# Moving the output transposes of a sliding-window attention two steps on, and a group's compressed scores to another PSUM place, in a two-block fp32 kernel

## What is computed

```
s = einsum('tghd,cgd->tghc', qt, k_cmp) * scale        # the compressed scores, 31 keys
p_cmp = masked_softmax(s, ...)
o_cmp = einsum('tghc,cgd->tghd', p_cmp, v_cmp)
...                                                     # o_slc, o_win in the same way over 512 keys
o = gt[:, 0] * o_cmp + gt[:, 1] * o_slc + gt[:, 2] * o_win
```

```
parts = [sink_col, s_ctx, where(band_ok, s_lat, NEG_INF)]
p = softmax(concatenate(parts))
o = einsum(p_ctx, vc) + einsum(p_lat, vb)               # (128 tokens) x (16 heads x 64)
```

## Time and profile before

| | us |
|---|---|
| median of 3 runs | 3192.96 |
| lowest and highest | 3188.86 and 3198.78 |
| the profiled execution's own time | 3198.71 |
| its span, first to last instruction | 3196.6 |
| mean granted TensorE clock in it | 0.975 |

### The profile page before, as it was taken

One profiled execution on the slowest core, in us unless ns is written; L12 is line 12 of the kernel. 1 busy time (PEld: TensorE's weight loads), 2 busy tenths in 40 slices (PEclk: granted clock), 3 DMA queues, 4 the chain that ended last, 5 costly groups with the idle time before them and its releaser, 6 DMA issues.

```text
span 3196.6 us, 41132 instructions
## 1 busy us (share of the span) xinstructions
PE 3018.4 (94%) x16349; PEld 2571.3 (80%) x16349; DVE 1659.3 (52%) x2849; ACT 1178.3 (37%) x2056; POOL 286.5 (9%) x274
## 2 busy tenths in 40 slices
PE   7999999887889999999888999999999999999999
PEld 5788888765778888887677888888888889888887
DVE  7767666668676666641445744222222655343333
ACT  4632223435673322331444643211112545442222
POOL 2410001001562000010000110000000100010001
PEclk9999999998999999999998999999999999899999
DMA  4235444242003444421000101111111210022231
GB/s 141 95 111 171 149 161 145 86 147 79 1 1 106 145 162 155 158 80 43 9 19 26 32 33 58 64 62 64 62 66 61 62 32 1 27 86 98 88 104 67
DMA packets 76286, 260.19 MB, mean 81 GB/s; under 512 B 8256, under 2 KB 12864, under 8 KB 75968
## 3 DMA queue, kind: packets, MB, share of 16 engines
q1 hardware_dynamic: 76096, 257.57, 24.1%
HBM read 255.44 MB, written 2.10 MB: 81 GB/s over the span
## 4 chain that ended last, share of the span: by engine, by line
PE 49%; DVE 3%; ACT 3%; issue 2%; DVEq 0%; ACTq 0%
PE PS L517 47%; PE PS L1416 2%; DVE SM L2450 0%; PE PS L1450 0%; ACT TMP L1423 0%; DVE PS L2250 0%; DVE SM L2120 0%; ACT TMP L1407 0%; ACT WH L439 0%; DVE QRS L1905 0%; DVE NKL L2174 0%; ACT PB L1423 0%; ACT PB L1407 0%; ACT N L2159 0%; DVE WL L445 0%
## 5 line engine op out<-in xcount | busy, mean ns | idle before, releaser
L439 ACT ACTIVATE WH<-RAW 128x1024 fp32r<-128x1024 f32 (+1 forms) x367 | 379.5, 1037 | 843.9 <-PE PS L517 557.6
L517 PE MATMUL PS<-UH,WH 128*128 128x512 f32 (+1 forms) x1664 | 602.4, 362 | 33.0 <-DVE UL L971 12.7
L445 DVE TENSOR_TENSOR WL<-RAW,WH 128x1024 fp32r<-128x1024 f32 (+1 forms) x367 | 446.4, 1220 | 340.2 <-ACT WH L439 329.3
L517 PE MATMUL PS<-UL,WH 128*128 128x512 f32 (+1 forms) x1664 | 590.7, 355 | 0.0
L517 PE MATMUL PS<-UH,WL 128*128 128x512 f32 (+1 forms) x1664 | 588.0, 353 | 0.0
L517 PEld LDWEIGHTS PS<-UH,WH 128*128 128x128 f32 x1664 | 317.6, 191 | 89.0 <-issue 16.3
L517 PEld LDWEIGHTS PS<-UL,WH 128*128 128x128 f32 x1664 | 317.5, 191 | 47.6 <-issue 5.9
L517 PEld LDWEIGHTS PS<-UH,WL 128*128 128x128 f32 x1664 | 316.4, 190 | 45.2
L658 POOL TENSOR_TENSOR ACC<-ACC,TMP 128x256 f32<-128x256 f32 (+1 forms) x108 | 117.6, 1104 | 2091.5 <-ACT TMP L648 2090.1
L517 PE MATMUL PS<-XSH,WH 128*128 128x512 f32 (+1 forms) x752 | 284.2, 378 | 5.2 <-ACT TMP L815 2.5
L517 PE MATMUL PS<-XSL,WH 128*128 128x512 f32 (+1 forms) x752 | 283.1, 376 | 0.0
(11 more groups left out here) (350 smaller groups left out, 5383.7 us busy)
## 6 DMA issues: line engine op xcount, KB each, us to landing
RAW<-in_mod_w SPq DMA_DIRECT2D x96, 512.0 KB, 3.3
RAW<-in_f_in SPq DMA_DIRECT2D x88, 512.0 KB, 3.4
RAW<-in_g_in SPq DMA_DIRECT2D x88, 512.0 KB, 3.2
RAW<-in_f_out SPq DMA_DIRECT2D x32, 448.0 KB, 3.8
RAW<-in_g_out SPq DMA_DIRECT2D x32, 448.0 KB, 3.1
RAW<-in_a_in SPq DMA_DIRECT2D x16, 512.0 KB, 3.9
RAW<-in_f_out SPq DMA_DIRECT2D x16, 512.0 KB, 4.0
RAW<-in_g_out SPq DMA_DIRECT2D x16, 512.0 KB, 3.2
```

What stands on the lines that cost most here:

```text
L439: act.e.activation(hi, raw, ACT.Copy).then_inc(wh.step(n, i), 1)
L445: dve.e.tensor_tensor(lo, raw, hi.bitcast(F32), ALU.subtract).then_inc(wl.step(n, i), 1)
L517: return pe.e.matmul(out, l, r, start=start, stop=stop)
```

## The change

In the sliding-window attention, `flip_tensor`, `flip_high` and `flip_low` of a query block go from step n+4 to step n+6, n being its last unit; the loops of the engines run to step 69 (before, PE and ACT to step 68 and DVE to step 67). `OST2` becomes two buffers of 1024 columns, at another address; a block's first output waits for the transposes of the block two before.

In the sparse attention, the compressed scores are made in the "aux" place that query blocks 1 and 3 use, in two pieces: the mask and the products of query blocks 0 and 1 (five) at the end of step n-3, those of query blocks 2 and 3 (four) at the end of step n-2. The first group's stay in one piece. ACT's copy to `CS` stays where it was.

```diff
-    OST2 = at("OST2", U0 + 44 * KB, [128, 1024])
+    OST2 = at("OST2", U0, [128, 2, 1024])
...
-         "score": [("lin", 0), ("lin", 1)], "across": [("lin", 2)], "half": [("half", 0), ("half", 1)]},
+         "score": [("lin", 0), ("lin", 1)], "across": [("lin", 2)], "half": [("half", 0), ("half", 1)], "compressed": [("aux", 0)]},
...
-        nsa_compressed(pe, 0)
+        psum.rings["compressed"] = [psum.rings["aux"][(psum.turn["aux"] + 1) % 2]]
+        nsa_compressed(pe, 0, (0, 1, 2, 3))
...
+            if s + 3 in CMP[1:]:
+                nsa_compressed(pe, s + 3, (0, 1))
             if s + 2 in CMP[1:]:
-                nsa_compressed(pe, s + 2)
-
-    def nsa_compressed(pe, n):
+                nsa_compressed(pe, s + 2, (2, 3))
+
+    def nsa_compressed(pe, n, blocks):
...
         g = NW[n].g
-        o = psum.enter("half", "compressed", g)
-        pe.wait_ge(*psum.clear("compressed", g), act_q.after("kp", 1), dve_q.after("nsa", 2 * g + 1, 1, "lo"))
-        mm(pe, o[:, 0:512].rearrange("p (t n) -> p t n", t=4), IDR[:, :], CMR[:, :].unsqueeze(1).to_broadcast([128, 4, 128]), True, False)
-        for q in range(4):
+        if blocks[0] == 0:
+            o = psum.enter("compressed", "compressed", g)
+            pe.wait_ge(*psum.clear("compressed", g), act_q.after("kp", 1), dve_q.after("nsa", 2 * g + 1, 1, "lo"))
+            mm(pe, o[:, 0:512].rearrange("p (t n) -> p t n", t=4), IDR[:, :], CMR[:, :].unsqueeze(1).to_broadcast([128, 4, 128]), True, False)
+        o = psum.at["compressed", g]
+        for q in blocks:
             c, x = slice(96 + 128 * g - 32 * q, 224 + 128 * g - 32 * q), Q2[:, q, 4 * g:4 * g + 4, :]
             mm(pe, o[:, 0:512], KPH[:, c], x, False, False)
             last = mm(pe, o[:, 0:512], KPL[:, c], x, False, q == 3)
-        last.then_inc(score.step("compressed", g), 1)
+        last.then_inc(score.step("compressed", g, blocks[-1]), 1)
...
-        for s in range(len(SWA) + 5):
+        for s in range(len(SWA) + 6):
...
-            n = s - 4
+            n = s - 6
             if 0 <= n < len(SWA) and SWA[n][1] == 15:
-                flip_tensor(pe, ("swa", SWA[n][0]), OST2, 8, [fin.after("swa", n)])
+                flip_tensor(pe, ("swa", SWA[n][0]), OST2[:, SWA[n][0] % 2, :], 8, [fin.after("swa", n)])
...
-                dve.wait_ge(outp.after("swa", n), recip.after("swa", n), *([flip.after(("swa", q - 1), 4)] if q else []))
+                dve.wait_ge(outp.after("swa", n), recip.after("swa", n), *([flip.after(("swa", q - 2), 4)] if q > 1 else []))
...
-                if h == 15:
-                    flip_low(dve, ("swa", q), flipped_hi(q), flipped_lo(q), 8)
+            n = s - 6
+            if 0 <= n < len(SWA) and SWA[n][1] == 15:
+                q = SWA[n][0]
+                flip_low(dve, ("swa", q), flipped_hi(q), flipped_lo(q), 8)
```

More of the change, by code:

```diff
@@ L1664, in compressed_scalar @@
     def compressed_scalar(act, g):
-        act.wait_ge(score.after("compressed", g), *([score.after("nsa", CMP[g - 1])] if g else []))
+        act.wait_ge(score.after("compressed", g, 3), *([score.after("nsa", CMP[g - 1])] if g else []))
         act.e.activation(CS[:, :], psum.at["compressed", g][:, 0:512], ACT.Copy).then_inc(act_q.step("compressed", g), 1)
@@ L2444, in swa_vector @@
     def swa_vector(dve):
-        for s in range(len(SWA) + 4):
+        for s in range(len(SWA) + 6):
             n = s - 1
@@ L2459, in swa_vector @@
                 q, h = SWA[n]
-                dve.wait_ge(outp.after("swa", n), recip.after("swa", n), *([flip.after(("swa", q - 1), 4)] if q else []))
-                dve.e.tensor_scalar(OST2[:, 64 * h:64 * h + 64], psum.at["outp", "swa", n][:, 0:64], stat_of(n)[:, 4:5], None,
+                dve.wait_ge(outp.after("swa", n), recip.after("swa", n), *([flip.after(("swa", q - 2), 4)] if q > 1 else []))
+                dve.e.tensor_scalar(OST2[:, q % 2, 64 * h:64 * h + 64], psum.at["outp", "swa", n][:, 0:64], stat_of(n)[:, 4:5], None,
                                     ALU.mult).then_inc(fin.step("swa", n), 1)
                 psum.leave(("outp", "swa", n), fin)
-                if h == 15:
-                    flip_low(dve, ("swa", q), flipped_hi(q), flipped_lo(q), 8)
+            n = s - 6
+            if 0 <= n < len(SWA) and SWA[n][1] == 15:
+                q = SWA[n][0]
+                flip_low(dve, ("swa", q), flipped_hi(q), flipped_lo(q), 8)
     def tensor_engine(pe):
```

## The result

| | before | changed |
|---|---|---|
| median of 11 runs, us | 3195.26 | 3185.85 |
| lowest and highest | 3180.76 and 3204.75 | 3180.84 and 3204.29 |
| profiled execution, span | 3196.6 | 3188.2 |

The ratio is 0.9969, with a 95% interval of 0.9955 to 0.9983: 9.4 us between the medians, where no difference was forecast. The measured median lies 0.15 us under the range.

A forecast was written before the change was run, and what follows sets the result against it. The prediction took PE to bound the kernel, busy 3018.4 of 3196.6 us. Last attention 0, first attention -0.9, clock +1.6 gave +0.7 us on a median of 3192.96: about 3193.7 us, range 3186 to 3201.

The forecast's parts named there:

- new wait of 2.5 us: First attention, three group boundaries: PE stops before the five products until DVE's `SUM` frees the "aux" place, about 2.5 us.
- small gain of 0.2 to 0.4 us a boundary: First attention: waits of 1.22 and 1.24 us go, one of 2.5 comes; 0.3 us gained at each of three boundaries, 0.9 in all.
- two of three boundaries fall: First attention: PE's clock drops at two group boundaries instead of one, +1.6 us; bounds -1.6 and +3.1.
- The removed wait ... was met already: worth 0: Last attention: the output transposes did not wait for DVE's last scaling, so removing that wait gains 0 us.
- 1.50 and 0.73 us: Last attention: PE's waits before the second four output transposes and before the next transposes stay, two steps later; worth 0.
- Rival 3: First attention: DVE's sum is done before PE asks, 1.24 us saved three times, no clock fall; 3187.7 us, chance 0.05.
- The term that stood at 0: Last attention: moving the output transposes two steps changes nothing, 0 us in the sum.
- 3 low stretches behind them: Last attention, sign to look for: three stretches at the low clock behind the moved output transposes.
- Rival 1: Last attention: the clock stays up after the moved output transposes, up to 12.5 us come back; chance 0.10.
- The price per us at the low clock: Last attention: 0.41 us lost of each us at the low clock, from steps of 2.10 and 3.54 us.
- Rival 2: Last attention: low-clock stretches behind the first two blocks' transposes do not end, 12.6 us more, 3206 us; chance 0.08.
- theory D: From the experiments, last attention: low-stretch length depends on its starting moment, handed on between blocks; added work moves low-clock time over 40 us.

The follow-up runs named there:

- nsa_only: Only the compressed scores moved to the "aux" place in two pieces, last attention as before, against the kernel before; 3197.92 us, ratio 1.0005.
- swa_only: Only the last attention's output transposes moved to n+6, with the double buffer, against the kernel before; 3186.95 us, ratio 0.9979.
- n+7: Output transposes three steps later than in the kernel before, with the double buffer, first attention as before; 3192.67 us, ratio 0.9988 to the kernel before.
- rep_4: Last attention made six times in one pipeline with two output buffers, transposes at n+4, against the kernel before; 4068.05 us.
- rep_6: As rep_4, with the output transposes at n+6 instead of n+4; 4016.94 us.
- six-fold kernel: The kernel before with its last attention made six times in one pipeline, 24 query blocks instead of four; 4068.05 us at n+4, 4016.94 at n+6.
- rep_4_pad2: Against rep_4, head 8's unit in each block makes its first two score products ten times more; 4094.35 us, 272 us at the low clock.
- rep_4_pad: Against rep_4, head 8's unit in each block makes its first two score products five times more; 4064.58 us, 278 us at the low clock.

## Why the prediction was wrong

**The parts that held.** The "**new wait of 2.5 us**": 2.26, ended by `SUM`, at all three boundaries (6.8 us in three waits). The small gain of 0.2 to 0.4 us a boundary: 0.36. "I take it that two of three boundaries fall instead of one": so it was, though it was a guess between bounds, in each of the three profiles with the new placing. The stage was forecast at +0.7 us; the two profiles differ by 0.3, and `nsa_only` is 1.0005 of before. "The removed wait ... was met already: worth 0" and the stay of the 1.50 and 0.73 us: as the waits show. Rival 3, no new wait, is out.

**The step that failed** is the one left out of the sum: the clock in the last attention. The text says that the idle pattern before each low stretch "is kept", and took from this that the low-clock time is kept too, apart from luck of an execution; the 5.8 us between the profiled execution and the median were put down to that luck and set aside. The term that stood at 0 measures -7.1 us (mean of three profiles each) and -7.3 us (`swa_only`, the stage's part alone). The sign named for it, "3 low stretches behind them", failed in all three profiles at n+6, which have one each (at n+4 they have 3, 3 and 2). The base was off too: the median of the kernel before is 3195.26 us in the 11 runs, not the 3192.96 of three, so the forecast of +0.7 us stands against -9.4, and the range was missed by only 0.15 us since its base lay 2.3 us too low. Rival 1 named the place and a price of up to 12.5 us, with the right sign, and had a chance of 0.10. The sentence that was for it, "the length of the stretches differs by six times for the same pattern, so they hang on little", deserved more weight: what they hang on is, as far as the runs show, the moment of the waits, and a move by two steps moves the moment. That the new moment would be a better one could not be read from the one trace; n+7 went the other way.

**The price per us at the low clock**, 0.41, held nearly: 0.37 between rep_4 and rep_6.

**Rival 2**, stretches that do not end, is real as a mechanism: a stretch of 47.8 us was seen in rep_4, at the old step. The changed kernel seems to meet something of the kind in some executions: 4 of its 23 runs took 3202.5 to 3205.7 us at a granted clock of 0.970 or 0.971, which is about 50 us more at the low clock than in the others. In which stage, no profile shows, since none was taken of these four; the kernel before has such runs too (up to 3208.28 us at 0.970), while of the 12 of `swa_only` none was over 3194 us.

The Trainium skill ("TensorE: Matmul & The Clock Gate", section "Why this matters for your kernels") sets a longer idle gap than this and would have left the clock up at the new wait of the first attention. Two of three boundaries fell after 2.26 us of idle time, in each of the three profiles, so here the measurement decides against the rule.

The same page, section "A second HAM failure mode: psum-queue depth-cycling", says that short pauses of PE between groups of products, made by turning through PSUM places, can make the clock swing. The last attention agrees: no wait in it is longer than 1.7 us, and 24 groups of waits of 1.5 us and less of rep_4 were followed by stretches of up to 47.8 us.

**Left open.** Which property of the work in a step lets a stretch end was not tested by itself: the table shows that the length follows from the distance over part of its range, and no run varied the outputs' 64-column products or the width of the keys' window. Nor was it tried whether the six-fold kernel with idle time added, instead of work, behaves as D says. Why rep_4_pad2 and rep_4_pad have the same low-clock time is open. So theory D is the best account of the runs and not proven: that the moment is handed on was read from the profiles, and no kernel's time was foretold from it.

## What to carry to other kernels

When PE is nearly full and runs at two clocks, a change that keeps every wait can still be worth several us by the clock; count the stretches at the low clock in several profiles, and compare the granted clock over all runs, before calling them luck, and repeat the stage in one kernel if a profile holds too few. A gain of this kind belongs to the position and not to the edit: in the six-fold kernel 20 us of work, spread over its 24 blocks, took it away. Breaking up a group of waits may last longer: there, two waits of 1.2 to 1.3 us with 2.5 us of work between them cost less clock (154 us at 1.2 GHz in the program) than 1.5 and 0.7 with 1.4 us between them at the best position (207). That was tried at one position only.

## What the runs showed of the hardware

The kernel before and the kernel with the edit have the same waits and within 1.5 us the same idle time in the last attention, yet differ by 7 us, which is granted clock. A stretch at 1.2 GHz can hold for 47.8 us while PE is busy for every one of them. It lay mostly in the dense small products of the fourth block's steps, whose length at that clock is 3.54 us. And a kernel of 4068 us took no longer with about 20 us of full-rate work added, as the time at the low clock sank from 344 to 278 us (4 runs each), while the same addition made one of 4017 us 52 us slower, with 82 us more at the low clock.
